# The prompt's mixing and queries with the activations stationary

## Chip, cores and metric

One core of a Trainium2 chip. The metric is the device time of one execution in microseconds: 2652.05 us is the median of three executions of the kernel before.

## What is computed

One layer of a hybrid backbone in f32, for 128 prompt tokens (one tile, tile 0) and 512 latent tokens (tiles 1 to 4) that share their weights. Cut to what the change touches, per token:

```python
h  = rmsnorm(x) * (1 + sc1) + sh1
y  = (sigmoid(h @ w_ga) * (o_a @ w_oa) + sigmoid(h @ w_gb) * (o_b @ w_ob)) @ w_out   # all D = 1024 wide
x  = x + gt1 * y
h2 = rmsnorm(x) * (1 + sc2) + sh2
q  = (h2 @ w_q).reshape(n, 8, 2, 128)              # 8 heads, two halves of 128
s  = einsum('nhpd,hpkd->nhpk', q, sub_keys)        # 128 keys for each half
# top 16 of each half, top 16 of their sums: 16 experts per head and token
x  = x + gt2 * sum over heads, k of softmax * gelu(u[idx] . h2) * v[idx]
```

`o_a` is a gated linear recurrence, `o_b` attention; both come before. The experts' rows are gathered from HBM, 128 per token.

## The kernel before

The five engines each run one program, written out by hand and joined by semaphores. The order is: modulation, norms and transposes of all five tiles; then everything of the prompt up to its scores (`scan(0)`, `attention([0])`, `mix(0)`, `post(0)`, L829 to L832 on TensorE); then the latent tiles (`win_turned`, `win`, four scans, attention, `mix(1)`, `post(1)`, `post(2)`). Beside the latent stages the prompt's 128 expert slots run: GpSimd gathers a row, VectorE takes a dot product, ScalarE forms the weight, VectorE adds the row to `pl`. Where each slot goes between the matmul groups is worked out beforehand from `STAGES` (L80) and the list of groups (`plan_groups`, L99). From `post(1)` on the latent tiles' slots follow. None of them can start before the prompt's scores: VectorE routes right after `post(0)` (L1645 to L1647).

**PSUM groups.** Each group of matmuls has a name in `plan_groups` and gets one or two of four banks of `pa` in turn. TensorE waits in `start` for the bank to be free, and `finish` marks the group full. A wide group (`x2T`, `h2`) takes two banks, and a pad is put in if its first bank number would be odd.

**Weights.** SyncE loads them as slabs of 256 weight columns (128 x 2048 f32, 1024 KB) into three slots in turn, in the order of the list `SLABS` (L88). A `wpq` slab also carries the two heads' halves of keys (128 x 256, so 1152 KB). The refill of a slot waits until the last group that reads its slab is full:

```python
if n >= NSLAB:
    wait_full(sp, last_use(SLABS[n - NSLAB]))       # L491, NSLAB = 3
"wo": ("rb", b, 2 * q + 1), ... "wpq": ("ss", b, 2 * q + 1)   # in last_use
```

**Mixing, `mix(0)`** (L751). The weights are stationary, 128 columns at a time, and the activations move: `hTp`, h transposed, 128 tokens wide. For each of four q, so 256 output columns: `gate_a` and `gate_b`, two halves m of 8 matmuls each; then for both m `ra` and `rb`, 4 matmuls each (the recurrence's and the attention's output against `w_oa` and `w_ob`). The results are transposed, features on the partitions. ScalarE applies the sigmoid to the gates (L1022), VectorE multiplies and adds (L1585, L1586) into `MT`, which is the stationary operand of the output projection.

**`post(0)`** (L780). Output projection `y`, 8 matmuls of 256 columns for each of four slabs, with `MT` stationary; VectorE applies the gate and adds (L1599, L1600); norm; eight transposes `x2T`, ScalarE scales and shifts (L935); eight transposes `h2`. Then the queries, 16 halves m, two to a slab: `qp(m)`, 8 matmuls of 128 columns with the weights stationary; ScalarE copies it to `QP`, which is transposed as the scores need it (L1039); `ss(m)`, one matmul against the keys; VectorE copies the scores (L1612). `qp(m+1)` is issued ahead of `ss(m)`.

In the profile `EB,RING` is `hTp` with a slab, `HG` holds the mixing's and the queries' working tiles, `R` the scores, `L570` is the helper of every matmul and `L573` that of every transpose. An f32 matmul leaves two records, a transpose one.

Of the kernel before, what the change touches and what calls it, by code (L numbers as in the profile page):

```python
# [98 lines left out]
def plan_groups():  # L99
# [20 lines left out]

    def mix(b):
        names.extend(("oT", t) for t in MIXES[b])
        for q in range(4):
            names.extend(("gate_a", b, 2 * q + m) for m in range(2))
            names.extend(("gate_b", b, 2 * q + m) for m in range(2))
            for m in range(2):
                names.extend([("ra", b, 2 * q + m), ("rb", b, 2 * q + m)])

    def post(b):
        tiles = BATCHES[b]  # L130
        names.extend(("y", q, t) for q in range(4) for t in tiles)
        for t in tiles:
            names.extend([("x2T", t), ("h2", t)])
        names.append(("qp", b, 0))
        for m in range(2 * PH):
            if m + 1 < 2 * PH:
                names.append(("qp", b, m + 1))
            names.append(("ss", b, m))
# [73 lines left out]
def build(nc, x_prompt, x_sample, cols, rows, normf_rows, brow, consts, masks, sel, cond_rows, ada_slabs, col_slabs, in_slabs, o_slabs,  # L212
          out_slabs, pq_slabs, uv, state, ckT, cv, y_prompt, y_sample, new_state, new_k, new_v):
    with ExitStack() as ctx:
# [90 lines left out]
        CKT, CV = view(HG, 0, 256), view(HG, 256, 2, P)  # L305


        NB, NM = ([len(t) * P for t in x] for x in (BATCHES, MIXES))
        OTA = [view(HG, 0, 4, P), view(AB, 0, 4, LAT)]
        OTB = [view(HG, 512, 4, P), view(AB, 10240, 4, LAT)]  # L310
# [39 lines left out]
        def psum(name):  # L350
            banks = PLACE[name][0]
            return (PA[:, 512 * banks[0]:512 * (banks[-1] + 1)] if banks[0] < 4
                    else PO[:, 512 * (banks[0] - 4):512 * (banks[0] - 3)])
# [19 lines left out]
        nst_ready, ctx_in = sem("nst_ready"), sem("ctx_in")  # L373
        qkT_ready, sm_ready, p_ready, pT_ready, ob_ready = (sem("qkT_ready"), sem("sm_ready"), sem("p_ready"),
                                                            sem("pT_ready"), sem("ob_ready"))
        pn_ready, oT_ready, sig2_ready, m_ready = sem("pn_ready"), sem("oT_ready"), sem("sig2_ready"), sem("m_ready")
        h2T_ready, h2_ready, qp_ready = sem("h2T_ready"), sem("h2_ready"), sem("qp_ready")
        kv_out, state_out, y_out, nf_in, zb_ready = (sem("kv_out"), sem("state_out"), sem("y_out"), sem("nf_in"),
# [92 lines left out]
        def _(sp):  # L471
            def last_use(key):
                kind = key[0]
                if kind == "ada":
                    return key
                if kind in ("winT", "winTL"):
                    return ("winP" if kind == "winT" else "winT", key[1], 2 * key[2] + 1)
                if kind in ("win", "winL"):
                    return ("win", key[1], key[2], 0 if kind == "win" else NT - 1)
                b, q = key[1:]  # L480
                return {"gate_a": ("gate_a", b, 2 * q + 1), "gate_b": ("gate_b", b, 2 * q + 1),
                        "wo": ("rb", b, 2 * q + 1), "wout": ("y", q, BATCHES[b][-1]),
                        "wpq": ("ss", b, 2 * q + 1)}[kind]
# [38 lines left out]
        def _(pe):  # L522
# [165 lines left out]
            def attention(tiles):  # L688
# [54 lines left out]
                for n in range(lo, hi + 3):  # L743
# [4 lines left out]
                    if n - 3 >= lo:  # L748
                        values(n - 3)

            def mix(b):  # L751
                tiles, N = MIXES[b], NM[b]
                pe.wait_ge(oa_ready, 1 if b == 0 else NT)
                for t in tiles:
                    ps = start(("oT", t))
                    for k in range(4):
                        last = tr(ps[:, k * P:(k + 1) * P], OA(t)[:, k * P:(k + 1) * P])
                    finish(("oT", t), last)
                for q in range(4):
                    for name in ("gate_a", "gate_b"):  # L760
                        w = chunks(slab(name, b, q))
# [17 lines left out]

            def post(b):  # L780
                tiles, N = BATCHES[b], NB[b]
                pe.wait_ge(m_ready, KD * (min(b, 1) + 1))
                for q in range(4):
                    w = chunks(slab("wout", b, q))
                    for t in tiles:
# [5 lines left out]
                for t in tiles:  # L791
                    pe.wait_ge(xn_ready, NT + t + 1)
                    ps = start(("x2T", t))
                    for k in range(KD):
                        last = tr(ps[:, k * P:(k + 1) * P], xn2(t)[:, k * P:(k + 1) * P])
                    finish(("x2T", t), last)
                    pe.wait_ge(h2T_ready, t + 1)
                    ps = start(("h2", t))
                    for k in range(KD):
                        last = tr(ps[:, k * P:(k + 1) * P], h_tile(t, k))  # L800
                    finish(("h2", t), last)

                def queries(m):
                    w = chunks(slab("wpq", b, m // 2))
# [62 lines left out]
        def _(act):  # L867
# [137 lines left out]
            def mix(b):  # L1005
# [6 lines left out]
                if b == 1:  # L1012
                    for t in tiles:
                        act.dma_start(X1[t], x_sample[(t - 1) * P:t * P, :]).then_inc(xr_in, 16)
                for q in range(4):
                    if q:
                        beside.before(("rb", b, 2 * q - 1))
# [6 lines left out]
            def post(b):  # L1024
                tiles, N = BATCHES[b], NB[b]
                for i, t in enumerate(tiles):
# [5 lines left out]
                        act.wait_ge(state_out, 32)  # L1032
                    ps = group(("h2", t))
                    step(A(H2[t], ps, ACT.Copy), *freed(("h2", t)), h2_ready)
                for m in range(2 * PH):
                    ps = group(("qp", b, m))
                    if m >= 2:
# [186 lines left out]
        def _(dve):  # L1224
# [350 lines left out]
            def mix(b):  # L1575
                tiles, N = MIXES[b], NM[b]

                for q in range(4):
                    for m in range(2):
                        n = 2 * q + m  # L1580
                        for a, name in enumerate(("ra", "rb")):
                            ps = group((name, b, n))
                            dve.wait_ge(sig2_ready, 16 * b + 4 * q + 2 * a + m + 1)
                            dst = SAB[b][a][:, m, :]
                            step(V.tensor_tensor(dst, ps[:, 0:N], dst, ALU.mult), *freed((name, b, n)))  # L1585
                        step(V.tensor_tensor(MT[b][:, n, :], SAB[b][0][:, m, :], SAB[b][1][:, m, :], ALU.add), m_ready)  # L1586
# [1 line left out]
            def post(b):  # L1588
# [14 lines left out]
                for i, t in enumerate(tiles):  # L1603
                    beside.before(("x2T", t))
                    if i > 1:
                        wait_full(dve, ("x2T", t - 2))
                    normed(NT + t, X1[t], xn2(t))
                for m in range(2 * PH):
                    ps = group(("ss", b, m))
                    ms = slice(m * NKEYS, (m + 1) * NKEYS)  # L1610
# [169 lines left out]
```

## Time and profile before

| | us |
|---|---|
| Median of three executions | 2652.05 (2648.12 to 2655.1) |
| The profiled execution | 2658.92 |
| Its span, first to last instruction | 2657.1 |
| TensorE, VectorE busy | 2044.4 (77%), 1736.2 (65%) |
| ScalarE, GpSimd busy | 970.5 (37%), 947.4 (36%) |
| Moved by DMA | 805.69 MB, 303 GB/s over the span |
| Mean granted TensorE clock | 0.910 of full |

The profiled execution is 6.9 us above the median and 1.8 us above its own span. Busy shares are averages over stages with different limits, so the rows below are taken from the stretch that the change touches and from what follows it.

### The profile page before, as it was taken

The page shows a single profiled execution, that of the slowest core. Times are in us where ns is not written, and L with a number is a line of the kernel's source. Part 1 is how long each engine was busy: PE and PEld are TensorE (multiplying, and loading weights), DVE is VectorE, ACT ScalarE, POOL GpSimd, SP SyncE. Part 2 cuts the span into 40 slices and gives each one's busy share as a digit, 9 for nine tenths or more (in the row PEclk, how much of TensorE's full clock was granted, in tenths as well). Part 3 has the DMA queues.
Part 4 walks back from the last instruction along what each step waited for, and adds up shares of the span by engine and source line. Part 5 has one row for each costly group of instructions (what it writes and reads, how often), then busy time and mean ns, then how long its engine had stood idle before and what let it go on. Part 6 is the DMA issues. An engine that isn't in the chain of part 4 may idle for free. (4 is left out here: it accounts for less than half of the span.)

```text
span 2657.1 us, 27312 instructions
## 1 busy us (share of the span) xinstructions
PE 2044.4 (77%) x6925; PEld 1127.9 (42%) x6925; DVE 1736.2 (65%) x3917; ACT 970.5 (37%) x2487; POOL 947.4 (36%) x806
## 2 busy tenths in 40 slices
PE   6969898855556799967689776878878777787776
PEld 2668746645545543355445322322223222232222
DVE  3632277765656668756768777777767667676674
ACT  1412153330035553421333343444434444344443
POOL 0020022632311113302123454566645555454454
PEclk9988998977868699978789999999999999999999
DMA  8835588830023368967679899999999999999997
GB/s 316 293 124 191 210 318 312 302 128 1 17 99 120 118 257 331 348 222 266 275 288 397 337 421 421 385 422 422 422 414 405 421 394 410 407 392 407 389 422 307
DMA packets 113319, 805.69 MB, mean 303 GB/s; under 512 B 12596, under 2 KB 14006, under 8 KB 17046
## 3 DMA queue, kind: packets, MB, share of 16 engines
q0 software_dynamic: 93760, 680.96, 64.0%
q1 hardware_dynamic: 17704, 118.17, 12.1%
q10 hardware_dynamic: 1712, 4.98, 0.5%
q8 instruction: 50, 0.82, 0.1%
q14 instruction: 93, 0.76, 0.1%
HBM read 800.79 MB, written 3.28 MB: 303 GB/s over the span
## 5 line engine op out<-in xcount | busy, mean ns | idle before, releaser
L1100 POOL DMA_INDIRECT RG<-in_uv,idxs x264 | 352.1, 1334 | 551.0 <-DVE pl L1351 318.8
L879 ACT ACTIVATE agel<-apre 128x1 f32<-128x1 f32 x640 | 129.1, 202 | 936.1 <-DVE apre L1323 929.5
L545 PE MATMUL pl<-RG,BP 128*128 128x512 f32 x576 | 294.1, 638 | 106.5 <-ACT BP L895 105.9
L545 PE MATMUL pl<-RING,BP 128*128 128x512 f32 x576 | 290.5, 640 | 81.0 <-ACT BP L895 79.8
L570 PE MATMUL pa<-HL,RING 128*128 128x512 f32 (+2 forms) x960 | 310.3, 480 | 6.2 <-DVEq L404 3.3
L1323 DVE CUSTOM_DVE_ANT_0 R<-RG,AB 128x1024 f32<-128x1024 f32 x201 | 246.4, 1229 | 97.1 <-DMA RG<-in_uv,idxs 77.3
L1100 POOL DMA_INDIRECT RING<-in_uv,idxs x168 | 227.8, 1356 | 204.9 <-PE pl L545 129.1
L1323 DVE CUSTOM_DVE_ANT_0 R<-RING,AB 128x1024 f32<-128x1024 f32 x168 | 205.8, 1225 | 118.0 <-DMA RING<-in_uv,idxs 74.2
L570 PEld LDWEIGHTS pa<-HL,RING 128*128 128x128 f32 x960 | 163.1, 192 | 145.7 <-issue 113.1
L545 PEld LDWEIGHTS pl<-RG,BP 128*128 128x128 f32 x576 | 100.2, 192 | 292.5 <-ACT BP L895 217.1
L545 PEld LDWEIGHTS pl<-RING,BP 128*128 128x128 f32 x576 | 108.6, 200 | 256.8 <-ACT BP L895 157.6
L895 ACT ACTIVATE BP<-CT,wexp 128x128 f32<-128x128 f32 x480 | 192.7, 402 | 56.8 <-PE pl L545 19.6
L885 ACT ACTIVATE wexp<-agel,gws 128x1 f32<-128x1 f32 x640 | 188.8, 295 | 22.6 <-ACT agel L879 0.8
L1100 POOL DMA_INDIRECT EB<-in_uv,idxs x88 | 112.5, 1279 | 205.7 <-DVE pl L1351 145.9
L1351 DVE SCALAR_TENSOR_TENSOR pl<-RG,wexp,pl 128x1024 f32<-128x1024 f32 x118 | 151.6, 1284 | 9.2 <-ACT wexp L885 9.1
L1323 DVE CUSTOM_DVE_ANT_0 R<-RG,BP 128x1024 f32<-128x1024 f32 x96 | 118.7, 1236 | 55.7 <-DMA RG<-in_uv,idxs 34.6
L570 PE MATMUL pa<-RING,HL 128*128 128x256 f32 x448 | 109.4, 406 | 26.0 <-ACTq L404 25.9
L879 ACT ACT_TABLE_LOAD x96 | 123.2, 1283 | 13.5 <-ACT HG L1022 3.0
L570 PE MATMUL pa<-HG 128*128 128x128 f32 (+1 forms) x576 | 84.7, 303 | 50.4 <-POOLq L1155 42.7
L1323 DVE CUSTOM_DVE_ANT_0 R<-EB,AB 128x1024 f32<-128x1024 f32 x67 | 82.3, 1228 | 57.3 <-DMA EB<-in_uv,idxs 55.5
L545 PE MATMUL pl<-HL,BP 128*128 128x512 f32 x192 | 94.3, 613 | 22.6 <-ACT BP L895 22.3
L570 PEld LDWEIGHTS pa<-RING,HL 128*128 128x128 f32 x448 | 90.3, 205 | 45.5 <-ACTq L404 25.6
(254 smaller groups left out, 3263.2 us busy)
## 6 DMA issues: line engine op xcount, KB each, us to landing
RING<-in_in_slabs SPq DMA_DIRECT2D x42, 1024.0 KB, 5.4
RING<-in_pq_slabs SPq DMA_DIRECT2D x24, 1152.0 KB, 6.1
RING<-in_ada_slabs SPq DMA_DIRECT2D x16, 1024.0 KB, 5.5
RING<-in_out_slabs SPq DMA_DIRECT2D x12, 1024.0 KB, 5.0
RG<-in_col_slabs POOLq DMA_DIRECT2D x8, 1024.0 KB, 7.1
RING<-in_o_slabs SPq DMA_DIRECT2D x8, 1024.0 KB, 4.9
RG<-in_uv,idxs POOLq DMA_INDIRECT x297, 12.1
RING<-in_uv,idxs POOLq DMA_INDIRECT x168, 14.5
```

The source lines that it names most:

```text
L545: last = nc.tensor.matmul(acc[:, c * 512:(c + 1) * 512], DG[:, k % 2, :], bufs[k % len(bufs)][:, D + c * 512:D + (c + 1) * 512], start=Fal ...
L570: return nc.tensor.matmul(out, l, r, start=s, stop=e)
L879: A(agel[:, par, k:k + 1], apre[:, par, k:k + 1], ACT.Gelu).then_inc(gel_done, 1)
L885: A(wexp[:, par, k:k + 1], agel[:, par, k:k + 1], ACT.Copy, scale=gws[:, par, k:k + 1]).then_inc(w_done, 1)
L895: A(DG[:, i % 2, :], ident, ACT.Copy, scale=wexp[:, par, k:k + 1]).then_inc(dg_done, 1)
L1100: nc.gpsimd.indirect_dma_start(out=bufs[b], out_offset=None, in_=uv, in_offset=bass.IndirectOffsetOnAxis(ap=idxs[:, par, k:k + 1], axis=0) ...
L1323: V.tensor_tensor_reduce(out=SCR[k % 2], in0=buf[:, 0:D], in1=hc, scale=1.0, scalar=0.0, op0=ALU.mult, op1=ALU.add, accum_out=apre[:, par, ...
L1351: V.scalar_tensor_tensor(PL[:, :], (GC[i % NGC] if t else GA[n % NGA])[:, D:2 * D], wexp[:, n // TOPK % 2, n % TOPK:n % TOPK + 1], PL[:, : ...
```

## The change

For the prompt alone (`b == 0`) the activations are the stationary operand and 256 weight columns move. The results come out with tokens on the partitions. In the mixing a q is then one group each of `gate_a`, `gate_b`, `ra` and `rb`, and the mixed rows, now in `M0`, are transposed by TensorE in two groups `mT` of four; ScalarE copies them to `MT`. In the queries a slab is one group `qp` of 8 matmuls, copied by ScalarE to `Q0`; two transposes `qT`, copied by VectorE to `QT0`; and one group `ss` of two score matmuls, copied 256 wide. A round i of the new loop issues `qp(i)`, `qT(i-1)`, `ss(i-2)`. The rest is left as it was, the latent tiles' parts among it. Left out of the diff are two new semaphores, `mT_ready` and `q0_ready`.

```diff
@@ -120,6 +120,12 @@
 
     def mix(b):
         names.extend(("oT", t) for t in MIXES[b])
+        if b == 0:
+            for q in range(4):
+                names.extend((kind, 0, q) for kind in ("gate_a", "gate_b", "ra", "rb"))
+                if q > 1:
+                    names.append(("mT", 0, q - 2))
+            return
         for q in range(4):
             names.extend(("gate_a", b, 2 * q + m) for m in range(2))
             names.extend(("gate_b", b, 2 * q + m) for m in range(2))
@@ -131,6 +137,12 @@
         names.extend(("y", q, t) for q in range(4) for t in tiles)
         for t in tiles:
             names.extend([("x2T", t), ("h2", t)])
+        if b == 0:
+            for i in range(PH + 2):
+                names.extend([("qp", 0, i)] if i < PH else [])
+                names.extend([("qT", 0, i - 1)] if 0 < i <= PH else [])
+                names.extend([("ss", 0, 2 * i - 3)] if i > 1 else [])
+            return
         names.append(("qp", b, 0))
         for m in range(2 * PH):
             if m + 1 < 2 * PH:
@@ -305,6 +317,7 @@
         CKT, CV = view(HG, 0, 256), view(HG, 256, 2, P)
 
 
+        M0, Q0, QT0 = view(HG, 3072, D), view(HG, 4608, 2, 256), view(HG, 5120, 2, 256)
         NB, NM = ([len(t) * P for t in x] for x in (BATCHES, MIXES))
         OTA = [view(HG, 0, 4, P), view(AB, 0, 4, LAT)]
         OTB = [view(HG, 512, 4, P), view(AB, 10240, 4, LAT)]
@@ -478,6 +492,8 @@
                 if kind in ("win", "winL"):
                     return ("win", key[1], key[2], 0 if kind == "win" else NT - 1)
                 b, q = key[1:]
+                if b == 0 and kind in ("gate_a", "gate_b", "wo"):
+                    return ("rb" if kind == "wo" else kind, 0, q)
                 return {"gate_a": ("gate_a", b, 2 * q + 1), "gate_b": ("gate_b", b, 2 * q + 1),
                         "wo": ("rb", b, 2 * q + 1), "wout": ("y", q, BATCHES[b][-1]),
                         "wpq": ("ss", b, 2 * q + 1)}[kind]
@@ -748,6 +764,60 @@
                     if n - 3 >= lo:
                         values(n - 3)
 
+            def turn_m(i):
+                pe.wait_ge(m_ready, 4 * (i + 1))
+                ps = start(("mT", 0, i))
+                for k in range(4):
+                    last = tr(ps[:, k * P:(k + 1) * P], M0[:, (4 * i + k) * P:(4 * i + k + 1) * P])
+                finish(("mT", 0, i), last)
+
+            def mix_prompt():
+                for q in range(4):
+                    for name in ("gate_a", "gate_b"):
+                        w = chunks(slab(name, 0, q))
+                        ps = start((name, 0, q))
+                        for k in range(KD):
+                            last = mm(ps[:, 0:SC_W], hTp[:, k, :], w[:, k, :], k == 0, k == KD - 1)
+                        finish((name, 0, q), last)
+                    w = slab("wo", 0, q)[:, 0:SLAB].rearrange("p (a k n) -> p a k n", a=2, k=4)
+                    if q == 0:
+                        pe.wait_ge(oT_ready, 1)
+                        pe.wait_ge(ob_ready, 1)
+                    ps = start(("ra", 0, q))
+                    for k in range(4):
+                        last = mm(ps[:, 0:SC_W], OTA[0][:, k, :], w[:, 0, k, :], k == 0, k == 3)
+                    finish(("ra", 0, q), last)
+                    ps = start(("rb", 0, q))
+                    for k in range(4):
+                        last = mm(ps[:, 0:SC_W], OTB[0][:, k, :], w[:, 1, k, :], k == 0, k == 3)
+                    finish(("rb", 0, q), last)
+                    if q > 1:
+                        turn_m(q - 2)
+
+            def queries_prompt():
+                for i in range(PH + 2):
+                    if i < PH:
+                        w = chunks(slab("wpq", 0, i))
+                        ps = start(("qp", 0, i))
+                        for k in range(KD):
+                            last = mm(ps[:, 0:SC_W], hTp[:, k, :], w[:, k, :], k == 0, k == KD - 1)
+                        finish(("qp", 0, i), last)
+                    if 0 < i <= PH:
+                        pe.wait_ge(q0_ready, i)
+                        ps = start(("qT", 0, i - 1))
+                        for k in range(2):
+                            last = tr(ps[:, k * P:(k + 1) * P], Q0[:, (i - 1) % 2, k * P:(k + 1) * P])
+                        finish(("qT", 0, i - 1), last)
+                    if i > 1:
+                        j = i - 2
+                        keys = slab("wpq", 0, j)[:, SLAB:SLOTW]
+                        pe.wait_ge(qp_ready, 2 * j + 2)
+                        ps = start(("ss", 0, 2 * j + 1))
+                        for k in range(2):
+                            last = mm(ps[:, k * P:(k + 1) * P], QT0[:, j % 2, k * P:(k + 1) * P],
+                                      keys[:, k * NKEYS:(k + 1) * NKEYS])
+                        finish(("ss", 0, 2 * j + 1), last)
+
             def mix(b):
                 tiles, N = MIXES[b], NM[b]
                 pe.wait_ge(oa_ready, 1 if b == 0 else NT)
@@ -756,6 +826,9 @@
                     for k in range(4):
                         last = tr(ps[:, k * P:(k + 1) * P], OA(t)[:, k * P:(k + 1) * P])
                     finish(("oT", t), last)
+                if b == 0:
+                    mix_prompt()
+                    return
                 for q in range(4):
                     for name in ("gate_a", "gate_b"):
                         w = chunks(slab(name, b, q))
@@ -779,7 +852,10 @@
 
             def post(b):
                 tiles, N = BATCHES[b], NB[b]
-                pe.wait_ge(m_ready, KD * (min(b, 1) + 1))
+                if b == 0:
+                    pe.wait_ge(mT_ready, 2)
+                else:
+                    pe.wait_ge(m_ready, KD * 2)
                 for q in range(4):
                     w = chunks(slab("wout", b, q))
                     for t in tiles:
@@ -799,6 +875,10 @@
                     for k in range(KD):
                         last = tr(ps[:, k * P:(k + 1) * P], h_tile(t, k))
                     finish(("h2", t), last)
+
+                if b == 0:
+                    queries_prompt()
+                    return
 
                 def queries(m):
                     w = chunks(slab("wpq", b, m // 2))
@@ -1012,6 +1092,18 @@
                 if b == 1:
                     for t in tiles:
                         act.dma_start(X1[t], x_sample[(t - 1) * P:t * P, :]).then_inc(xr_in, 16)
+                if b == 0:
+                    for q in range(4):
+                        act.wait_ge(m_ready, 2 * q)
+                        for a, name in enumerate(("gate_a", "gate_b")):
+                            ps = group((name, 0, q))
+                            step(A(SAB[0][a].rearrange("p a n -> p (a n)"), ps[:, 0:SC_W], ACT.Sigmoid),
+                                 *freed((name, 0, q)), sig2_ready)
+                        if q > 1:
+                            ps = group(("mT", 0, q - 2))
+                            step(A(MT[0][:, 4 * (q - 2):4 * (q - 1), :], ps.rearrange("p (k n) -> p k n", k=4), ACT.Copy),
+                                 *freed(("mT", 0, q - 2)), mT_ready)
+                    return
                 for q in range(4):
                     if q:
                         beside.before(("rb", b, 2 * q - 1))
@@ -1032,6 +1124,13 @@
                         act.wait_ge(state_out, 32)
                     ps = group(("h2", t))
                     step(A(H2[t], ps, ACT.Copy), *freed(("h2", t)), h2_ready)
+                if b == 0:
+                    for i in range(PH):
+                        ps = group(("qp", 0, i))
+                        if i > 1:
+                            wait_full(act, ("qT", 0, i - 2))
+                        step(A(Q0[:, i % 2, :], ps[:, 0:SC_W], ACT.Copy), *freed(("qp", 0, i)), q0_ready)
+                    return
                 for m in range(2 * PH):
                     ps = group(("qp", b, m))
                     if m >= 2:
@@ -1575,12 +1674,21 @@
             def mix(b):
                 tiles, N = MIXES[b], NM[b]
 
+                if b == 0:
+                    for q in range(4):
+                        s2 = [x.rearrange("p a n -> p (a n)") for x in SAB[0]]
+                        for a, name in enumerate(("ra", "rb")):
+                            ps = group((name, 0, q))
+                            dve.wait_ge(sig2_ready, 2 * q + a + 1)
+                            step(V.tensor_tensor(s2[a], ps[:, 0:SC_W], s2[a], ALU.mult), *freed((name, 0, q)))
+                        step(V.tensor_tensor(M0[:, q * SC_W:(q + 1) * SC_W], s2[0], s2[1], ALU.add), m_ready, m_ready)
+                    return
                 for q in range(4):
                     for m in range(2):
                         n = 2 * q + m
                         for a, name in enumerate(("ra", "rb")):
                             ps = group((name, b, n))
-                            dve.wait_ge(sig2_ready, 16 * b + 4 * q + 2 * a + m + 1)
+                            dve.wait_ge(sig2_ready, 8 * b + 4 * q + 2 * a + m + 1)
                             dst = SAB[b][a][:, m, :]
                             step(V.tensor_tensor(dst, ps[:, 0:N], dst, ALU.mult), *freed((name, b, n)))
                         step(V.tensor_tensor(MT[b][:, n, :], SAB[b][0][:, m, :], SAB[b][1][:, m, :], ALU.add), m_ready)
@@ -1605,6 +1713,15 @@
                     if i > 1:
                         wait_full(dve, ("x2T", t - 2))
                     normed(NT + t, X1[t], xn2(t))
+                if b == 0:
+                    for i in range(PH + 1):
+                        if i < PH:
+                            ps = group(("qT", 0, i))
+                            step(V.tensor_copy(QT0[:, i % 2, :], ps[:, 0:256]), *freed(("qT", 0, i)), qp_ready, qp_ready)
+                        if i:
+                            ps = group(("ss", 0, 2 * i - 1))
+                            step(V.tensor_copy(SC[0][:, (i - 1) * 256:i * 256], ps[:, 0:256]), *freed(("ss", 0, 2 * i - 1)))
+                    return
                 for m in range(2 * PH):
                     ps = group(("ss", b, m))
                     ms = slice(m * NKEYS, (m + 1) * NKEYS)
```

## Rows read from the trace of the kernel before

**Rows 1.** Stretches: length; busy (x) of PE, PEld, DVE, ACT, POOL; clock; DMA share; GB/s
```profile
217.10:261.50 44.40, 43.52 (x387) 43.33 (x385) 7.00 (x24) 7.60 (x19) 0.00 (x0) 0.99 0.77 261
...
287.50:323.00 35.50, 33.93 (x290) 33.38 (x288) 4.64 (x16) 6.27 (x18) 0.00 (x0) 0.97 0.61 214
323.00:406.00 83.00, 82.64 (x192) 36.40 (x192) 65.68 (x158) 36.96 (x63) 20.78 (x19) 1.00 0.80 301
```

**Rows 2.** The page's head: the span
```profile
span 2657.1 us, 27312 instructions
```

**Rows 3.** VectorE in order of time: start, length, engine, line, operation
```profile
323.53 0.91 DVE L1645 MEMSET pl<- 128x1024 f32 x1 [0.51 <-DVE R L1612]
```

**Rows 4.** TensorE in order of time, the mixing and the output projection
```profile
228.29 7.31 PE L570 MATMUL pa<-EB,RING 128*128 128x128 f32 x64
235.44 3.74 PE L570 MATMUL pa<-HG,RING 128*128 128x128 f32 x32
...
261.50 14.08 PE L570 MATMUL pa<-RING,HG 128*128 128x256 f32 x64 [0.88 <-DVEq L404]
```

**Rows 5.** VectorE in order of time, the output projection's four groups
```profile
265.33 0.42 DVE L1599 TENSOR_TENSOR HG<-pa,EB 128x256 f32<-128x256 f32 x1 [3.95 <-PE pa L570]
265.90 0.43 DVE L1600 TENSOR_TENSOR XS<-XS,HG 128x256 f32<-128x256 f32 x1
...
275.69 0.42 DVE L1599 TENSOR_TENSOR HG<-pa,EB 128x256 f32<-128x256 f32 x1 [2.46 <-PE pa L570]
```

**Rows 6.** TensorE in order of time, the modulation
```profile
32.84 5.73 PE L570 MATMUL pa<-RING,condT 128*2 128x256 f32 x16 [7.07 <-DMA RING<-in_ada_slabs]
...
38.72 3.62 PE L570 MATMUL pa<-RING,condT 128*2 128x256 f32 x16
...
71.05 1.10 PE L573 MATMUL pa<-CT,HG 128*128 128x128 f32 x8
```

**Rows 7.** ScalarE in order of time: a copy of 512 columns, a latent group
```profile
217.43 0.60 ACT L1010 ACTIVATE HG<-pa 128x512 f32<-128x512 f32 x1 [2.01 <-PE pa L573]
...
351.32 0.60 ACT L1057 ACTIVATE AB<-pa 128x512 f32<-128x512 f32 x1
```

**Rows 8.** TensorE in order of time, the prompt's queries
```profile
287.55 4.79 PE L570 MATMUL pa<-EB,RING 128*128 128x128 f32 x32
292.18 0.39 PE L570 MATMUL pa<-RING,HG 128*128 128x128 f32 x2
292.40 1.95 PE L570 MATMUL pa<-EB,RING 128*128 128x128 f32 x16
294.19 0.39 PE L570 MATMUL pa<-RING,HG 128*128 128x128 f32 x2
...
309.60 2.05 PE L570 MATMUL pa<-EB,RING 128*128 128x128 f32 x16 [0.96 <-DMA RING<-in_pq_slabs]
```

**Rows 9.** SyncE's queue in order of time: the issue of two slabs
```profile
294.60 0.33 SPq L503 DMA_DIRECT2D RING<-in_pq_slabs  x1
302.64 0.33 SPq L503 DMA_DIRECT2D RING<-in_pq_slabs  x1
```

**Rows 10.** Line 503 in 294 to 295 us, then 302 to 303 us: landing
```profile
DMA to landing us min/median/max: 5.1/5.1/5.1
DMA to landing us min/median/max: 6.9/6.9/6.9
```

**Rows 11.** The stretch behind the wait of 7.07 us, columns as in rows 1
```profile
32.80:37.00 4.20, 4.16 (x10) 1.23 (x11) 0.00 (x0) 0.83 (x1) 0.00 (x0) 0.50 0.59 246
```

**Rows 12.** Who waited for whom, 406 to 560 us: total, times, longest
```profile
PE pa L570 <- ACTq L404: 25.9, 12, 4.0
...
PE pa L570 <- DVEq L404: 14.9, 1, 14.9
```

**Rows 13.** Instruction groups, 217 to 323 us: busy us, mean ns, idle before
```profile
L570 PE MATMUL pa<-EB,RING 128*128 128x128 f32 x512 | 61.9, 279 | 1.0 <-DMA RING<-in_pq_slabs 1.0
...
L570 PE MATMUL pa<-RING,HG 128*128 128x256 f32 x64 | 14.1, 381 | 0.9 <-DVEq L404 0.9
```

More of the change, by code:

```diff
@@ L375, in build @@
                                                             sem("pT_ready"), sem("ob_ready"))
+        mT_ready, q0_ready = sem("mT_ready"), sem("q0_ready")
         pn_ready, oT_ready, sig2_ready, m_ready = sem("pn_ready"), sem("oT_ready"), sem("sig2_ready"), sem("m_ready")
```

## The prediction

> **What bounds the kernel now.** The stage table [rows 1] says where to look. The changed stage runs from 217.1 to 323.0 us of a 2657.1 us span [rows 2]. Over its two parts that change, the mixing (217.1 to 261.5) and the queries (287.5 to 323.0), TensorE is busy 43.5 of 44.4 us and 33.9 of 35.5 us, VectorE and ScalarE some 5 to 8 us in each. So TensorE bounds both, and the expert slots, which later keep VectorE and ScalarE going, have not begun. One end hands everything on: VectorE clears `pl` and begins the first route at 323.53 [rows 3], right behind the last score copy. What matters is by how much that moment moves.
>
> **The mixing.** 192 matmuls of 128 columns become 96 of 256, columns as before. The 32 matmuls of one q's gates take 7.15 us from start to start (228.29 to 235.44 [rows 4]; an f32 matmul leaves two records, hence x64), so one takes 0.2234 us and 192 take 42.9 us. For 256 columns the nearest rows are the output projection's: four groups of eight, VectorE taking them up at 265.33 and 275.69 [rows 5], so 10.36 / 24 = 0.432 us each; 96 take 41.5. That is -1.4 us. Weight loads halve, but they are hidden already: two 128-column matmuls cost 0.447 against 0.432.
>
> Added are 8 transposes, 4 behind q = 2 and 4 behind q = 3. Eight in a row took 1.10 us [rows 6], so 4 cost 0.54 (to the next start). The first four find their data ready (q 0 and 1 are long mixed) and add 0.54. The last four lie on the path: last `rb`, VectorE's product and sum of 256 columns (0.57 from start to start at 265.33 and 265.90 [rows 5], so 1.14 with the hand-over), transposes 0.54, ScalarE's copy of 512 columns 0.60 [rows 7], some 0.3 of hand-overs: 2.6 us. The old chain there took 0.88 [rows 4]: +1.7. Mixing in sum: -1.4 + 0.54 + 1.7 = **+0.8 us**. The slab queue keeps up: a slab is let go after 3.45 us of work instead of 3.57 and is needed 6.9 us after its issue, landings take about 5.1, and the projection already runs at that pace without a break [rows 4]. VectorE and ScalarE do fewer, wider steps beside TensorE, at no cost.
>
> **The queries: their work.** Before, eight slabs took 35.1 us, from 287.55 to 322.7: a round of eight matmuls and one `ss` is 292.18 to 294.19, 2.01 us [rows 8], and there are 16; 1.05 more went to a slow clock at the start, 0.96 to the one slab that came late, 0.9 to the last `ss`. After, a slab costs 8 x 0.432 = 3.46 for `qp`, 0.27 for two transposes, 0.45 for two score matmuls (0.22 each): 4.18, times 8 is 33.4. With the slow start 1.05 and a tail of 0.3 (the last `ss` waits for VectorE's copy of `qT`) that is 34.8. Work alone changes nothing (-0.3).
>
> **The queries: the ring.** The keys lie in the slab, and SyncE refills slot j % 3 with slab j+3 only once `ss` of slab j is full (L491, `last_use`). Before, that was half a slab into slab j+1, so a refill had one and a half slabs, 6 us, to land; issues at 294.60 and 302.64 landed in 5.1 and 6.9 us [rows 9, 10]. In the new loop round i issues `qp(i)`, `qT(i-1)`, `ss(i-2)`. Slab j is let go at the end of round j+2, and the next thing in TensorE's queue, `qp(j+3)`, wants the slab whose transfer has just been released. No work lies between: `ss` and `qT` that could run are queued behind `qp`. So rounds 3 to 7, five of them, each wait out a whole transfer: 0.02 to issue, 5.1 to land, 0.06 to the first matmul (302.64 + 6.9 against 309.60 [rows 8 to 10]). I take 5.1, since the transfer released at 294.60 began with nothing else under way, as each would here; the upper end is 6.9, with two in flight. Per round **+5.2 us**. Rounds 0 to 2 find slabs loaded during the projection.
>
> By the Trainium skill, "SBUF — State Buffer", The DMA setup-cost knee, a transfer takes a fixed 2 us and its bytes at 436 GB/s: 4.7 us estimated for these 1152 KB, where the trace has 5.1; the five waits would be 2 us less in sum.
>
> **The clock.** Idle TensorE falls from 2.4 to 1.2 GHz. After it had waited 7.07 us on a transfer, sixteen records of 128x256 took 5.73 us against 3.62 later [rows 6], granted clock 0.50 for the first 4.2 us of them [rows 11]. The slow start at 287.55 follows two idle stretches of 4 us. With 5.2 us idle in each round I expect the same: +2.1 us per round (nothing is the lower end; all of `qp` slow, 3.5, the upper). A round is then 5.2 + 3.46 + 2.1 + 0.27 + 0.45 = 11.5 us.
>
> **The sum.** Queries start at 288.35 (+0.8). Rounds 0 to 2: 3 x 3.46 + 2 x 0.27 + 0.45 + 1.05 = 12.4, to 300.8. Five rounds of 11.5: 358.1. Rounds 8 and 9: 0.27 + 0.45 + 0.3 + 0.45, to 359.6. Against 322.7 that is +36.9, and the last copy is 256 wide (+0.1): VectorE starts routing **37 us later**. ScalarE and GpSimd wait for VectorE's route and shift with it. TensorE's own queue is hit harder: the first latent slab now waits for round 7, lands near 363.3, so its first matmul comes about 40 us later and slow (2 more). That lag of 3 to 5 us I cost at nothing: TensorE runs 82.6 us without a stop from 323 [rows 1], ScalarE takes the second group away only at 351.32 [rows 7] though it was full near 336.9 (each of the 12 groups takes 6.9), and later TensorE waits 25.9 us for ScalarE and 14.9 for VectorE [rows 12]. The slots set that pace. If the cover failed it would cost 5 us more. Bank numbers behind the prompt rotate by 22 mod 4 = 2 with parity kept, so no pad changes: nothing. No later stage has a start that didn't move, so nothing is paid back.
>
> The profiled execution took 2658.9 us, the median is 2652.05; the difference is applied to the median: 2652.05 + 37 = **2689 us**.
>
> **Rivals.**
> *Stall without the slow clock* (chance 0.15). The wait is just 5.2 us, and if TensorE falls only near its end the cost shrinks. 37 - 5 x 2.1 = +26.5: 2678.5. Against it: 7.07 us of wait gave the fall, and 4 us waits precede the slow start at 287.55.
>
> *Stall, and the lag behind it isn't covered, or landings are nearer 6.9* (0.15). Lag +5, or 5 x 1.8 = +9: 2694 to 2698.
>
> *The ring keeps up; the change isn't slower* (0.07). Place: SyncE's refill of rounds 3 to 7. It decides at the point where slab j+3 lands before round j+3 begins, which needs the release a `qp` (3.5 us) earlier and a landing under 4.2. Then +0.8 - 0.3 = +0.5 us, 2652.5. The order of the queue speaks against it.
>
> *Weight loads do cost, and halving them pays* (0.03). Records read alone say so: 279 ns each at 128 columns, 381 at 256 as the groups of instructions give their mean length [rows 13], ratio 0.68. That would take 0.32 x (42.9 + 28.6) = 23 us off (128 matmuls of the queries cost 28.6); the work added gives 4.4 back (0.54 + 1.7 + 8 x 0.27), so with a ring that keeps up 2633.5. Starts [rows 4, 5] say 0.97, since the lengths overlap.
> By the Trainium skill, "TensorE: Matmul & The Clock Gate", Back-to-back issue gap, the load is part of the spacing (81 ns at N=128, 131 at N=512, so about 98 at 256 if interpolated, 0.60 of two at 128): that favours the change, and the trace doesn't bear it out.
>
> **How the numbers follow.** The forecast has 0.60, the rivals 0.15, 0.15, 0.07, 0.03. The two about the stall's size lie beside the forecast, and the range takes them in with the lower landing: 2675 to 2698. About 0.1 for no stall and a bit of each tail stay outside. 0.3% is 8 us, about what a measurement of this kernel can tell from no change: slower 0.9, within it 0.07, faster 0.03.
>
> **What would show it.** In the chain and the waits of the changed kernel: five waits of TensorE for `in_pq_slabs` in the prompt's queries, each near 5.1 us (rounds 0 to 2 none), `qp` groups of 5.5 us at clock 0.50 then 1.00, issues of slabs 3 to 7 some 11.5 us apart, the clearing of `pl` near 360.6, and the latent stages as long as before. Mixing should end with an idle chain of 2.6 us in two pieces. It would be wrong if the waits were short (ring), if `qp` took 3.5 us (clock), or if the stretch from the first route to the end grew or shrank by more than 5 us.

## The result, and the profile after

The changed kernel takes 2693.68 us (median of four executions, 2684.34 to 2696.24) where the kernel before takes 2653.57. The ratio is 1.0144 (95% interval 1.0118 to 1.017): 40 us slower, 37 were forecast, 2675 to 2698 was the range. The profiled execution after took 2684.34 us with a span of 2682.4, the shortest of its four, and that of the kernel before is 5 us above the median, so the gain or loss of a stage is read below from stage to stage and not from the two spans.

TensorE of the changed kernel in order of time, from the mixing's last group to the first latent group (start, length, engine, line, operation, idle before it and who ended that). These rows answer to [rows 4, 8]:

```profile
254.08 3.62 PE L586 MATMUL pa<-RING,HG 128*128 128x256 f32 x16
258.94 0.66 PE L589 MATMUL pa<-CT,HG 128*128 128x128 f32 x4 [1.24 <-DVEq L418]
260.41 15.77 PE L586 MATMUL pa<-RING,HG 128*128 128x256 f32 x64 [0.81 <-ACTq L418]
...
287.29 7.63 PE L586 MATMUL pa<-RING,EB 128*128 128x256 f32 x32
...
298.64 0.61 PE L586 MATMUL pa<-RING,HG 128*128 128x128 f32 x4
305.28 5.48 PE L586 MATMUL pa<-RING,EB 128*128 128x256 f32 x16 [6.03 <-DMA RING<-in_pq_slabs]
310.60 0.38 PE L589 MATMUL pa<-CT,HG 128*128 128x128 f32 x2
310.82 0.61 PE L586 MATMUL pa<-RING,HG 128*128 128x128 f32 x4
316.57 6.65 PE L586 MATMUL pa<-RING,EB 128*128 128x256 f32 x16 [5.14 <-DMA RING<-in_pq_slabs]
...
329.16 5.49 PE L586 MATMUL pa<-RING,EB 128*128 128x256 f32 x16 [5.28 <-DMA RING<-in_pq_slabs]
...
340.92 6.42 PE L586 MATMUL pa<-RING,EB 128*128 128x256 f32 x16 [5.61 <-DMA RING<-in_pq_slabs]
...
353.10 5.41 PE L586 MATMUL pa<-RING,EB 128*128 128x256 f32 x16 [5.09 <-DMA RING<-in_pq_slabs]
...
364.08 84.04 PE L586 MATMUL pa<-HL,RING 128*128 128x512 f32 x192 [2.53 <-issue]
```

Five waits for a query slab, 6.03, 5.14, 5.28, 5.61 and 5.09 us, 27.2 in sum, stand where one of 0.96 stood in [rows 8]. Each follows at once on an `ss` (the row `RING,HG` x4). Behind each the same eight matmuls take 5.4 to 6.7 us, against 3.46 from start to start at full clock.

Stretches of the changed kernel (length; busy and instructions of PE, PEld, DVE, ACT, POOL; clock; DMA share; GB/s), to be held against [rows 1]:

```profile
214.60:260.40 45.80, 43.76 (x201) 37.84 (x200) 5.10 (x12) 6.15 (x12) 0.00 (x0) 0.98 0.76 263
260.40:287.30 26.90, 18.64 (x81) 15.89 (x82) 5.70 (x13) 5.14 (x10) 0.00 (x0) 0.83 0.53 192
287.30:361.60 74.30, 46.46 (x177) 37.88 (x176) 6.38 (x16) 5.38 (x10) 0.00 (x0) 0.79 0.24 85
361.60:448.00 86.40, 83.92 (x193) 37.20 (x194) 68.26 (x164) 38.64 (x66) 21.53 (x20) 0.98 0.81 315
```

The queries are 74.3 us long instead of 35.2 (287.55 to 322.7). TensorE is busy 46.5 of them at a mean clock of 0.79, and the DMA engines idle for three quarters: the stage waits for transfers, one at a time, in a stretch with bandwidth to spare.

Cuts of one such round, a wait (299.25 to 305.28) and what follows. The number behind the five engines is the granted clock, 1.00 at 2.4 GHz and 0.50 at 1.2:

```profile
301.00:302.00 1.00, 0.00 (x0) 0.00 (x0) 0.00 (x0) 0.00 (x0) 0.00 (x0) 1.00 0.70 295
302.00:303.00 1.00, 0.00 (x0) 0.00 (x0) 0.00 (x0) 0.00 (x0) 0.00 (x0) 0.53 1.04 442
...
305.30:308.00 2.70, 2.70 (x6) 2.17 (x7) 0.00 (x0) 0.00 (x0) 0.00 (x0) 0.50 0.00 0
308.00:309.00 1.00, 1.00 (x4) 0.81 (x3) 0.00 (x0) 0.00 (x0) 0.00 (x0) 0.56 0.00 0
309.00:310.00 1.00, 1.00 (x7) 0.87 (x6) 0.00 (x0) 0.00 (x0) 0.00 (x0) 1.00 0.00 0
```

The clock fell to 1.2 GHz after some 3 us of the 6.03 us wait and came back when TensorE had been busy for some 3.6.

VectorE hands the rest of the kernel its start, as [rows 3] before:

```profile
362.52 0.91 DVE L1762 MEMSET pl<- 128x1024 f32 x1 [0.51 <-DVE R L1723]
```

Counted from the mixing's first matmul (217.12 before, 214.60 after) that is 147.9 us instead of 106.4: 41.5 us later. This stretch, from the mixing's first matmul to the clearing of `pl`, is called the prompt's stage below.

### The profile page after: what moved, and what is told of

Read it like the earlier page. It is cut to its first block and busy times, and to the rows that moved or that the text cites. A ratio compares the mean times of both kernels' runs of the same rounds, so it can differ in the third digit from the quotient of the medians.

```text
span 2682.4 us, 26653 instructions
## 1 busy us (share of the span) xinstructions
PE 2051.7 (76%) x6629; PEld 1123.4 (42%) x6629; DVE 1735.0 (65%) x3905; ACT 969.7 (36%) x2473; POOL 937.7 (35%) x806
## 5 line engine op out<-in xcount | busy, mean ns | idle before, releaser
L586 PE MATMUL pa<-RING,HL 128*128 128x256 f32 x448 | 103.1, 391 | 22.5 <-ACTq L418 22.5
L586 PE MATMUL pa<-RING,EB 128*128 128x256 f32 x368 | 94.4, 421 | 27.2 <-DMA RING<-in_pq_slabs 27.2
L561 PE MATMUL pl<-EB,BP 128*128 128x512 f32 x192 | 98.9, 639 | 14.5 <-ACT BP L975 14.5
```

The lines of the kernel that those rows point to most:

```text
L561: last = nc.tensor.matmul(acc[:, c * 512:(c + 1) * 512], DG[:, k % 2, :], bufs[k % len(bufs)][:, D + c * 512:D + (c + 1) * 512], start=Fal ...
L586: return nc.tensor.matmul(out, l, r, start=s, stop=e)
```

## The experiments

Theory (ring): the refill of a query slab waits for its scores, which TensorE takes just before it wants that slab, and the wait lets the clock fall. Rival (shape): the wide groups, extra transposes and hand-overs cost the time. A third question came up on the way: what happens behind the prompt.

**Keys apart (e1).** The prompt's keys go into a tile of their own (`RG`, idle at that time), and a query slab is let go when `qp` is full:

```diff
+                if b == 0 and kind == "wpq":
+                    return ("qp", 0, q)
...
+                if key == ("wo", 0, 0):
+                    sp.wait_ge(coldot_done, NCOL)
+                    sp.dma_start(RG[:, 0:8 * 256].rearrange("p (q k) -> p q k", q=PH),
+                                 pq_slabs[:, :, SLAB:SLOTW].rearrange("q p k -> p q k")).then_inc(keys_in, 16)
...
-                        keys = slab("wpq", 0, j)[:, SLAB:SLOTW]
+                        keys = RG[:, j * 256:(j + 1) * 256]
```

> The changed kernel, but the prompt's keys are loaded once into a tile of their own, and a query slab is let go when its qp is full. Ring theory: the five waits for slabs 3 to 7 (27 us in the changed kernel's trace) and the slow clock behind them (about 12 us) go, so the queries take about 35 us instead of 74 and the whole is 2 us above the kernel before (ratio 1.000 to 1.002). Shape theory (wide groups, extra transposes and hand-overs cost the time): the queries stay above 60 us and the ratio near 1.014.

A query slab without its keys is also smaller, 1024 instead of 1152 KB; e4 and e5 leave the size alone and tell that apart from the release.

Measured: 2652.47 us, ratio 0.9989 (0.9976 to 1.0001). Nothing is left of the loss in the total, and no wait for a slab in the queries. The prompt's stage takes 109.5 us (217.24 to 326.69), 3.0 more than before and 38.5 less than in the changed kernel. TensorE of this kernel in order of time:

```profile
302.60 3.62 PE L594 MATMUL pa<-RING,EB 128*128 128x256 f32 x16
306.05 0.38 PE L597 MATMUL pa<-CT,HG 128*128 128x128 f32 x2
306.27 0.61 PE L594 MATMUL pa<-RG,HG 128*128 128x128 f32 x4
306.72 3.62 PE L594 MATMUL pa<-RING,EB 128*128 128x256 f32 x16
```

A round is 4.12 us (302.60 to 306.72); 4.18 was reckoned. The shape theory is out for the queries.

**Mixing only (e2), queries only (e3).** The branches `b == 0` of the other part are taken out on all engines.

> Only the mixing is changed, the queries are as before. Ring theory: +2 us (the trace of the changed kernel has 45.8 us against 44.4 from the first gate to the output projection, and 1.7 more in the projection at a slow clock), ratio 1.000 to 1.002. Shape theory: a third to a half of the 40 us, ratio 1.005 or more.

> Only the queries are changed, the mixing is as before. Ring theory: the whole loss, 37 to 40 us, ratio 1.014 to 1.015, with five waits of 5 to 6 us. If the mixing carried a part, correspondingly less.

Queries only: 2690.89 us, ratio 1.0129 (1.0108 to 1.015), five waits of 25.3 us in sum, 5.03 to 5.14 each. The loss is the queries', as expected. Mixing only: 2642.27 us, ratio 0.9956 (0.994 to 0.9972). Slower by 2 was expected, and it is faster by 12, though the prompt's stage (215.64 to 323.95) is 1.9 us longer than before, just as expected. This gain lies behind the prompt; see below.

**The old kernel with a late release (e4).** Nothing is turned; only SyncE's wait moves:

```diff
+                if b == 0 and kind == "wpq":
+                    return ("ss", 0, min(2 * q + 4, 15))
```

> The kernel before with nothing turned: in the prompt's queries SyncE refills a slab only when ss(2j+4) is full, one and a half slabs later, so that qp(2j+6) wants it at once. Ring theory: five waits of 5.1 to 6 us and a slow clock behind each (2 us), 35 to 40 us in all, ratio near 1.014, though each matmul is as before. Shape theory: the old groups stay as fast, with at most some 10 us for the waits, ratio below 1.005.

Measured: 2687.56 us, ratio 1.0134 (1.0114 to 1.0155). Its TensorE in order of time:

```profile
301.23 0.39 PE L572 MATMUL pa<-RING,HG 128*128 128x128 f32 x2
306.67 3.78 PE L572 MATMUL pa<-EB,RING 128*128 128x128 f32 x16 [5.06 <-DMA RING<-in_pq_slabs]
310.24 0.64 PE L572 MATMUL pa<-RING,HG 128*128 128x128 f32 x2
310.67 2.19 PE L572 MATMUL pa<-EB,RING 128*128 128x128 f32 x16
```

The old matmuls with the late release lose most of what the change lost, 35.0 of 41.5 us in the prompt's stage (218.37 to 359.78): five waits, 25.3 us in sum. Behind the first, 5.06 us, eight matmuls take 3.78 us for what takes 1.95 in [rows 8]. So the release alone is enough, and with e1 (without it the change costs 3 us of the stage and nothing in the total) it is the cause.

**Scores ahead of the queries (e5).** A round is `ss(i-2)`, `qp(i)`, `qT(i-1)`; names and loop are reordered, nothing else.

> The changed kernel with a round's order turned: ss(i-2), qp(i), qT(i-1). A slab is let go one qp (3.5 us) and one qT (0.3) earlier against its use. Ring theory: each of the five waits falls from 5.4 to about 1.6 us, too short for the clock to fall, so 5 x (3.8 + 2.3) = 30 us come back: 8 to 12 us above the kernel before, ratio about 1.004. If the wait is set by something else than the release, it stays near 5 us and the ratio near 1.014.

Measured: 2659.9 us, ratio 1.0014 (0.9999 to 1.0029). The waits fell further than reckoned, to a single 0.21 us. In their place TensorE idles 0.81 us in each round ahead of `ss`. The profile names no releaser; by the program it is the copy of `qT`, which `ss` now follows at once. That idle time lies between release and use too:

```profile
308.36 0.38 PE L589 MATMUL pa<-CT,HG 128*128 128x128 f32 x2
309.56 0.68 PE L586 MATMUL pa<-RING,HG 128*128 128x128 f32 x4 [0.81 <-issue]
310.45 3.72 PE L586 MATMUL pa<-RING,EB 128*128 128x256 f32 x16 [0.21 <-DMA RING<-in_pq_slabs]
314.01 0.38 PE L589 MATMUL pa<-CT,HG 128*128 128x128 f32 x2
```

The clock stays up (3.72). `pl` is cleared at 334.78: from the transposes of `h2` on 47.7 us instead of 77.0, the 30 that were expected. The order of the loop alone gives back 29 of the 39 us that the queries had lost. The prompt's stage is 118.2 us, 11.8 more than before; the total is only 3.7 above, at most 7.7 by its interval, where 8 to 12 were expected. So some 4 us or more came back behind the prompt, for which this run gives no cause.

**Filling the wait (e6).** Behind each `ss` of slabs 0 to 4:

```diff
+                        if j < 5:
+                            for _ in range(5):
+                                mm(PL[:, 0:512], ident, M0[:, 0:512])
```

> The changed kernel with five f32 matmuls of 512 columns (4.3 us at full clock) of no use behind each ss of slabs 0 to 4, into pl, which VectorE clears later. They lie inside the wait for the slab. Clock theory: the waits' ends stay where they are, but qp then runs at the full clock, 3.6 us instead of 5.9, so about 5 x 2.3 = 11 us less than the changed kernel: ratio to before about 1.010. Rival (the longer qp comes from something else, as a slab whose bytes come late or its port): qp stays near 5.9 us, ratio 1.014 or above.

Measured: 2688.7 us, ratio 1.0116 (1.0088 to 1.0144). The wait's end stays and `qp` is fast again:

```profile
306.61 0.61 PE L586 MATMUL pa<-RING,HG 128*128 128x128 f32 x4
307.05 4.46 PE L586 MATMUL pl<-HG,CT 128*128 128x512 f32 x10
313.25 3.72 PE L586 MATMUL pa<-RING,EB 128*128 128x256 f32 x16 [1.74 <-DMA RING<-in_pq_slabs]
```

From `h2` to the clearing of `pl` it is 67.1 us instead of 77.0: the clock's share is 10 of the 39 us that the queries lost. The waits for slabs have 26 (27.2 less 0.96), and some 3 are left for the new round's transposes and its tail. TensorE still idled 1.74 us behind the first fill and 0.8 to 1.0 behind the others, and the clock stayed up. The total's interval takes in both 1.010 and the changed kernel's 1.0144, so it is the trace that decides here.

**Keys apart with the old mixing (e7), and with a warm tail (e8).** e8 adds to e1 one f32 matmul of 512 columns in each of the two short waits at the mixing's end.

> Queries changed, keys apart, mixing as before. Sum of parts: the queries' work alone, -0.3 us, less the one late slab (1 us) that the kernel before waits for, so 2652 to 2654 where before is 2653.6: ratio 0.999 to 1.001. If fewer weight loads paid by the length of the records, 0.996 or less.

> Keys apart with both parts changed, and one f32 matmul of 512 columns of no use (0.86 us) in each of the two short waits at the end of the mixing. In the changed kernel these two idle stretches of 1.2 and 0.8 us were followed by a slow clock in the output projection (15.8 us instead of 14.1). Clock theory: the projection takes 14.1 us again, 1.7 us less than with the keys apart alone. Rival: the fall there is a chance of that execution, and the projection takes 14.1 us in the other runs without the fill too.

e8: 2649.66 us, ratio 0.9983 (0.9966 to 0.9999). The output projection in e8, TensorE in order of time:

```profile
261.98 14.08 PE L594 MATMUL pa<-RING,HG 128*128 128x256 f32 x64
```

And the same in e1, without the fills:

```profile
262.44 15.77 PE L594 MATMUL pa<-RING,HG 128*128 128x256 f32 x64 [0.81 <-ACTq L418]
```

All seven kernels with the new mixing and no fills there (after, e1, e2, e5, e6, e9, e12) have 15.72 to 15.77 us, all with the old mixing 14.08, and the two fills, which leave 0.38 us idle, bring it back to 14.08. The granted clock of the changed kernel in its projection (begun at 260.41), columns as above:

```profile
261.00:262.00 1.00, 1.00 (x4) 0.81 (x3) 0.00 (x0) 0.70 (x1) 0.00 (x0) 0.55 0.78 320
262.00:263.00 1.00, 1.00 (x4) 0.75 (x3) 0.00 (x0) 0.00 (x0) 0.00 (x0) 0.50 0.00 0
```

So it wasn't chance: idle stretches of 1.24 and 0.81 us, 0.7 busy between them, were enough for the clock to fall, where 0.88 before [rows 4] was not. The totals of e1 and e8 (2.8 us apart) don't part them.

e7: 2644.86 us, ratio 0.9967 (0.9953 to 0.9981), 9 us faster where 1 was expected, close to what halved weight loads should have given. But the prompt's stage (217.95 to 324.68) takes 106.7 us against 106.4 before and 105.6 in e10, the old kernel with keys apart, so the gain isn't the queries' and lies behind the prompt again.

**What lies behind the prompt (e9 to e12).** e9 is e2 with keys apart, e10 the kernel before with keys apart. e11 is the kernel before with four matmuls of no use:

```diff
+                if b == 0:
+                    for _ in range(4):
+                        mm(PL[:, 0:P], ident, hTp[:, 0, :])
                 pe.wait_ge(m_ready, KD * (min(b, 1) + 1))
```

> Mixing changed, queries as before, keys apart. By its parts: mixing only (0.9956 measured) less the one late slab (1 us): 2641 us, ratio 0.995 to 0.996, if the 12 us that the mixing alone gained belong to the mixing. If they belong to how the slots of the later stages happen to fall in step in each build, the prompt's stage still ends within 2 us of the kernel before and the ratio lies anywhere from 0.995 to 1.001.

> The kernel before with the prompt's keys apart and nothing else. Its prompt stage can gain only the one late slab, 1 us: ratio 0.9995 to 1.000 by its parts. If the later stages' step differs from build to build, up to 10 us less or 3 more.

> The kernel before with four f32 matmuls of 128 columns of no use (0.9 us) in the 0.88 us in which TensorE waits before the output projection. By its parts nothing changes: ratio 1.000. A ratio below 0.998 or above 1.002 would mean that the later stages answer to a shift of a fraction of a microsecond or to the program's layout.

> The mixing-only kernel again, unchanged, with more executions. If its 12 us are a property of that build, the ratio is again 0.994 to 0.997, with the prompt's stage as long as before and the gain in the latent stages; if they were the luck of six executions, it comes back to 0.998 to 1.001.

Measured: e9 2639.96 us, 0.9947 (0.993 to 0.9964); e10 2652.64 us, 0.9988 (0.9973 to 1.0002); e11 2656.71 us, 1.0013 (0.9999 to 1.0026); e12 2639.82 us, 0.9944 (0.9926 to 0.9961). The gain of mixing only is no luck of six executions, as six further ones show it again, and the shift of a fraction of a microsecond in e11 didn't bring it. e9's total fits both readings of its expectation; its trace decides, since the prompt's stage takes 106.6 us against 106.4 before, and the mixing has gained nothing. Who waited for whom on VectorE shows where it is. The kernel before, from 1970 to 2640 us:

```profile
DVE R L1323 <- issue: 25.2, 6, 5.3
```

Mixing only, the same stretch:

```profile
DVE R L1406 <- issue: 12.1, 3, 5.6
```

Both are idle stretches inside the tile passes in which VectorE waits for nothing that the profile shows. The longest, 4.6 to 6.1 us each, stand in order of time where a pass loop (`Fori`, L1695; three rounds for each of tiles 2 to 4) goes round, so two in a tile that has them. The other two of the six are of 2.7 us, 5 us behind those of tile 4. The kernel before, tile 3:

```profile
2058.70 0.08 DVE L1323 DVE_READ_ACCUMULATOR2_ANT apre<- 128x1 f32 x1
2064.08 1.22 DVE L1323 CUSTOM_DVE_ANT_0 R<-RING,AB 128x1024 f32<-128x1024 f32 x1 [5.29 <-issue]
```

Which tiles have stops differs from build to build. The table has all 14 profiles. A tile's time is from the last step of the tile before (`tile_end`, L1637) to its own; the last column has the sum of the long stops:

| Kernels | Tile 2 | Tile 3 | Tile 4 | Long stops |
|---|---|---|---|---|
| before, after, e1, e4, e5, e6, e8, e10, e11 | 324.0 to 325.2 us | 334.7 to 335.9 | 333.9 to 335.1 | tiles 3 and 4: 19.9 to 21.3 us |
| e3, e7 | 334.2, 334.3 | 335.5, 334.6 | 324.3, 324.8 | tiles 2 and 3: 20.0, 20.1 |
| e2, e9, e12 | 324.0 to 324.9 | 324.7 to 325.0 | 332.3 to 334.7 | tile 4 alone: 10.8 |

A tile with stops takes 332 to 336 us and moves 17 or 18 packets of the instruction queue q14, a tile without 324 to 325 us and 7 or 8 packets, without exception. So e2, e9 and e12 owe some 10 of their 12 to 14 us to the loop of tile 3, which doesn't stop in them. In 2058 to 2066 us of the kernel before, around the stop shown, the DMA engines were all busy with expert rows (q0 at 101% of 16 engines) and q14 moved one packet. The pattern goes with the build and not with the execution: e2 and e12 are the same kernel, and e3 and e7 have nearly the same number of instructions (27064 and 27065), as have e2 and e9 (26901 and 26902). That the stops are VectorE fetching its own loop again is inferred from queue and place; no run here moved the loop alone. By the Trainium skill, "Runtime: NRT & Kernel Launch", Instruction fetch mechanics, a taken branch whose target lies outside the two pages held forces a fetch before execution goes on. The trace fits that rule, with 4.6 to 6.1 us a time.

The stops don't explain e7: its tiles 2 to 4 take 993.7 us together, those of the kernel before 995.1. From the clearing of `pl` to the end of tile 0, though, e7 takes 826.1 us where the kernel before takes 837.0. This stretch too differs among the kernels, with one profiled execution each: 837.0 to 838.7 in before, e10 and e11, 824.9 to 833.4 in the eleven others. What e7 gained probably lies there, and so may what came back in e5 and the rest of the gain of e2, e9 and e12; the cause stays open.

The fastest kernels of the study are e9 and e12, mixing changed and queries as before (e9 with keys apart too), 0.5% below the kernel before. The gain isn't the mixing's, whose stage is no shorter. If the stops depend on where the loop lies in the program, which was argued and not tested, it could go with the next edit.

## Why the prediction was right

37 us were forecast and 40 measured, but the interval of the total runs from 31 to 45 us, so the total alone proves little. The stage that was reckoned lost 41.5 us; what follows compares it term by term.

**The ring.** Right in place, number and size: five waits, rounds 3 to 7, none before. 5.2 us a round was taken, 5.43 measured (27.2 / 5). e4 and e1 show it from both sides. Landings near 6.9 us, half of the rival beside it, are out: the longest wait was 6.03. The rival in which the ring keeps up decides where it was said, as e5 shows, with a release 4.5 us earlier.

**The clock.** The mechanism held (e6). Its size was short: 2.1 us a round from the one row of [rows 6], where `qp` took 5.48, 6.65, 5.49, 6.42 and 5.41, so 5.89 on average with the overlap of some 0.15, 2.3 above 3.46. The rival without the slow clock is out; its price, 5 x 2.1, is close to the 10 us that e6 measured.

**The queries' work.** -0.3 us forecast. e1's round was 4.12 against 4.18, and its queries took 36.2 us (289.50 to 325.7), 1.0 more than before. 0.8 of that is a slower start, and the tail was 1.0 longer than reckoned: without the ring the turned queries gain nothing.

**The mixing.** +0.8 forecast, +1.4 measured (45.8 against 44.4). Matmuls from q to q take 10.36 us for 24 of them (226.02 to 236.38), 0.432 each as reckoned, and four transposes 0.43 where 0.54 was taken. The closing chain was 2.7 us against 2.6. What is over is the first group's slow start, 8.12 us for 16 matmuls against 7.07 at full clock, where before it was 7.76 against 7.31.

**The step that was missed.** The two idle pieces of that chain were costed as idle time alone. They also brought the clock down, and the output projection took 1.7 us longer; `x2T`, which then ran at full clock (1.09 us instead of 1.97), gave 0.9 back. With the mixing's 0.6, the waits' 1.1, the clock's 0.9 and a tail (`ss` of the last two slabs, 359.11 to 361.55) 1.0 longer than reckoned, that is nearly all of the 4.5 us between 41.5 and 37.

**The cover behind it.** TensorE's first latent matmul came 1.56 us behind the clearing of `pl` where it had been 0.39 ahead, a lag of 2 us and not of 3 to 5, since VectorE's start came later than reckoned too. From that clearing to the end of tile 0 the changed kernel took 824.9 us, the kernel before 837.0, so a cost of the lag doesn't show; with a spread of 14 us among the kernels in this stretch one of a few microseconds can't be excluded either.

**What was wrong behind the prompt.** The prediction named as a sign against itself that the stretch from the first route to the end shrinks by more than 5 us. In the two profiles it did: from the clearing of `pl` to the end of tile 4 it is 2315.5 us after and 2329.2 before, 13.7 less, of which 12.1 lie ahead of the end of tile 0. The medians don't show it: they are 40.1 us apart, the two clearings 39.0. As the executions of one kernel differ by 12 us (2648 to 2660, 2684 to 2696) and these two are a long one of the kernel before and the shortest after, the pair doesn't decide whether anything was paid back. As a rule "nothing is paid back" was wrong: in e2, e9 and e12 the loop of tile 3 alone gave back some 10 us, for a reason that no term of the sum had. That the total came out near the forecast is in part luck, since the changed kernel happened to keep its stops in the tiles where the kernel before had them.

**Weight loads.** The rival from the records' mean lengths (0.68) is out. The spacing in the mixing is 0.432 us for 256 columns against 0.447 for twice 128, a ratio of 0.97. The Trainium skill's "TensorE: Matmul & The Clock Gate", Back-to-back issue gap, gives 0.60 as an estimate, interpolated between its two figures; in this f32 kernel the measurement decides.

## What to carry to other kernels

When a loop is reordered, write down for each buffer of a ring the last reader and the next writer's user, and count what the engine has in its queue between them; a transfer needs its landing time there (5 us for 1152 KB), and three slots are worth nothing if the release stands right ahead of the use. A small operand that rides in a big slab keeps the whole slab alive; load it apart, or read it earlier. A wait of TensorE costs the wait and then a slow start (here 2.3 us on top of 5.4), and a difference of 0.5% between two builds may be neither's merit: compare the stages, and look at the waits for nothing where loops go round, before crediting the edit.

## What the runs showed of the hardware

TensorE's clock fell after two short waits of 1.24 and 0.81 us with 0.7 us of transposes between them, though not after one of 0.88 (before) nor after one of 1.74 behind 4.46 us of matmuls (e6), and e8's fills took that fall away. VectorE stopped for 4.6 to 6.1 us where a hardware loop went round, in some tiles and builds and not in others, in loops whose bodies were the same: two stops in a kernel or four, 10.8 to 21.3 us of 2650. The difference is more than any gain that this change could have brought.
